# Who makes the low parts of the seven quarter products: three subtractions per unit moved from GpSimd to VectorE

## The reference

```
x = x + 0.5 * (silu(h @ w_gate) * (h @ w_up)) @ w_down      h = rms_norm(x), w_gate and w_up 1024 x 2816
proj = h @ w_in ; x = x + (gate_a * branch_a + gate_b * branch_b) @ w_out
x = x + 0.5 * (silu(h @ w_gate) * (h @ w_up)) @ w_down      second feed-forward block, weights of its own
```

## Time and profile before

| | |
|---|---|
| median of three runs | 2593.43 us (2591.48 to 2594.05) |
| the profiled execution | 2593.64 us, its span 2591.8 us |
| PE busy | 2576.2 us, 99% of the span |
| DVE busy | 1408.8 us, 54% |
| ACT busy | 1147.6 us, 44% |
| POOL busy | 1122.9 us, 43% |

### The profile page before, as it was taken

How to read it: one execution, slowest core, us unless ns; L and a number is a source line. 1 busy time by engine, 2 the same in 40 slices (tenths; PEclk the granted TensorE clock), 3 DMA queues, 4 the chain that set the end, 5 groups by cost and what they waited for, 6 DMA issues and landing times.

```text
span 2591.8 us, 32921 instructions
## 1 busy us (share of the span) xinstructions
PE 2576.2 (99%) x13244; PEld 2165.6 (84%) x13244; DVE 1408.8 (54%) x1949; ACT 1147.6 (44%) x1691; POOL 1122.9 (43%) x458
## 2 busy tenths in 40 slices
PE   9999999999999999999999999999999999999999
PEld 7999887888876788988888988878888778898987
DVE  7777426751345357665187682458423453677630
ACT  5334336743546443334243342467445464433331
POOL 4434544455431334435434345434544314434353
PEclk9999999999999999999999999999999999999999
DMA  5322724323322332322324223343233232324232
GB/s 166 118 78 86 235 88 118 106 96 108 94 72 88 102 114 90 112 84 90 99 90 130 86 82 107 92 125 102 86 110 97 66 103 90 122 65 130 66 102 77
DMA packets 258669, 263.77 MB, mean 102 GB/s; under 512 B 9574, under 2 KB 243174, under 8 KB 258518
## 3 DMA queue, kind: packets, MB, share of 16 engines
q1 hardware_dynamic: 253178, 251.65, 31.3%
q10 hardware_dynamic: 5340, 10.02, 1.2%
HBM read 252.25 MB, written 10.57 MB: 101 GB/s over the span
## 4 chain that ended last, share of the span: by engine, by line
PE 90%; DVE 6%; ACT 2%; DMA 1%; issue 0%; ACTq 0%; SPq 0%; DVEq 0%
PE ps L1671 22%; PE ps L1676 22%; PE ps L1675 22%; PE ps L1779 5%; PE ps L1783 5%; PE ps L1784 5%; PE ps L1951 1%; DVE scan L1474 1%; PE ps L2009 1%; PE ps L2024 1%; PE ps L1969 1%; PE ps L1973 1%; PE ps L1974 1%; DVE scan L1466 1%; DVE scan L1471 1%; ACT i_and_r L854 0%
## 5 line engine op out<-in xcount | busy, mean ns | idle before, releaser
L579 POOL TENSOR_TENSOR wlo<-raw,whi 128x1024 fp32r<-128x1024 f32 x386 | 972.6, 2532 | 1032.6 <-ACT whi L623 1032.6
L1671 PE MATMUL ps<-h_lo,whi 128*128 128x512 f32 x1632 | 639.2, 392 | 3.6 <-DVE y L1406 2.8
L1675 PE MATMUL ps<-h_hi,whi 128*128 128x512 f32 x1632 | 636.5, 390 | 0.0
L1676 PE MATMUL ps<-h_hi,wlo 128*128 128x512 f32 x1632 | 636.4, 390 | 0.0
L623 ACT ACTIVATE whi<-raw 128x1024 fp32r<-128x1024 f32 x386 | 403.7, 1053 | 459.1 <-PE ps L1671 404.6
L1671 PEld LDWEIGHTS ps<-h_lo,whi 128*128 128x128 f32 x1632 | 307.4, 188 | 73.3 <-issue 9.2
L1676 PEld LDWEIGHTS ps<-h_hi,wlo 128*128 128x128 f32 x1632 | 307.1, 188 | 64.6
L1675 PEld LDWEIGHTS ps<-h_hi,whi 128*128 128x128 f32 x1632 | 307.4, 188 | 62.7
L1671 PE MATMUL ps<-act_lo,whi 128*128 128x512 f32 x704 | 274.1, 389 | 0.0
L1675 PE MATMUL ps<-act_hi,whi 128*128 128x512 f32 x704 | 273.9, 389 | 0.0
L1676 PE MATMUL ps<-act_hi,wlo 128*128 128x512 f32 x704 | 273.9, 389 | 0.0
(11 more groups left out here) (232 smaller groups left out, 4396.6 us busy)
## 6 DMA issues: line engine op xcount, KB each, us to landing
raw<-in_w_in SPq DMA_DIRECT2D x124, 512.0 KB
raw<-in_w_up SPq DMA_DIRECT2D x88, 512.0 KB
raw<-in_w_down SPq DMA_DIRECT2D x80, 512.0 KB
w_a<-in_w_gate SPq DMA_DIRECT2D x60, 512.0 KB, 5.0
tmp<-in_w_gate SPq DMA_DIRECT2D x20, 512.0 KB, 7.9
rel_band<-rel_rows ACTq DMA_DIRECT2D x1, 8192.0 KB, 39.5
raw<-in_w_up_b SPq DMA_DIRECT2D x16, 512.0 KB
raw<-in_w_out SPq DMA_DIRECT2D x16, 512.0 KB
```

The costliest lines, as they stand in the source:

```text
L579: nc.gpsimd.tensor_tensor(wlo[:, s, :], src, whi[:, s, :].bitcast(F32), ALU.subtract).then_inc(lo_made, 1)
L1671: ins = pe.matmul(ps[:, b, :], w_hi, x_lo, start=start, stop=False)
L1675: pe.matmul(ps[:, b, :], w_hi, x_hi, start=False, stop=False)
L1676: return pe.matmul(ps[:, b, :], w_lo, x_hi, start=False, stop=stop)
```

## The change

VectorE makes the low parts of all seven operands of a unit's quarter products; POOL makes those of the four up chunks alone. A11's low part comes before that of S2, A12's (with the wait for A12's load ahead of it) before that of S1, and A22's after the sum that waits for P5. The counts follow: `sum_lo` steps by seven a unit (PARTS is 7), all seven products wait for it, `lo_made` steps by four, and SP waits for `sum_lo` alone before it loads the next quarters. ACT's two waits in the last unit are for the same two low parts as before under new counts.

```
 SP      if unit:
-            sp.wait_ge(sum_lo, ((2 * l + f) * UNITS + unit) * 4)
-            sp.wait_ge(lo_made, lows[0] - UPS)
+            sp.wait_ge(sum_lo, ((2 * l + f) * UNITS + unit) * PARTS)
...
-        lows[0] += 3
 POOL    for unit in range(UNITS):
-            base = ring[0]
             plain(UPS)
-            lo(w_a11[:, :])
-            ring[0] = base + RING_A12
-            lo(w_a12)
-            ring[0] = base + RING_A22
-            lo(w_a22[:, :])
+            ring[0] += PARTS
 ACT     if last:
-            act.wait_ge(sum_lo, C.now(sum_lo) + 2)
+            act.wait_ge(sum_lo, C.now(sum_lo) + 4)
...
-            act.wait_ge(sum_lo, C.now(sum_lo) + 4)
+            act.wait_ge(sum_lo, C.now(sum_lo) + 6)
 DVE     (two up tiles scaled, unless last)
+            lo_sum(base + RING_A11, w_a11[:, :])
             lo_sum(base + RING_S2, w_s2[:, :])
         (two more up tiles scaled, unless last)
+            dve.wait_ge(held_loaded[3], C.next(held_loaded[3], 16))
+            lo_sum(base + RING_A12, w_a12)
             lo_sum(base + RING_S1, w_s1[:, :])
-            dve.wait_ge(held_loaded[3], C.next(held_loaded[3], 16))
...
             added(u4, p5, u2).then_inc(bank_read[p5], C.made(bank_read[p5]))
+            lo_sum(base + RING_A22, w_a22[:, :])
             if last:
                 act_low(2, 4)
 PE
-    seventh(chunk(), p1, *of_h(low, left))
-    seventh(sum_chunk(sums + 1), p6, *of_t(T2, 1))
...
+    seventh(sum_chunk(sums + 1), p1, *of_h(low, left))
+    seventh(sum_chunk(sums + 2), p6, *of_t(T2, 1))
...
+    seventh(sum_chunk(sums + 7), p4, *of_t(T4, 4))
```

More of the change, by code:

```diff
@@ L751, in ffn @@
                     C.step(sum_made, 4)
-                    C.step(sum_lo, 4)
+                    C.step(sum_lo, PARTS)
                     sums = C.now(sum_made)
@@ L1123, in down_low @@
             def down_low(l, f, n):
-                first = 4 + UNITS * (UPS + 3)
+                first = 4 + UNITS * UPS
                 block = first + (KD // 2) * len(G22)
@@ L1797, in strassen @@
                 p1, p6, p2, p5, p7, p3, p4 = GATE_BANKS
-                seventh(chunk(), p1, *of_h(low, left))
-                seventh(sum_chunk(sums + 1), p6, *of_t(T2, 1))
[L1800 to L1805, removed]
+                seventh(sum_chunk(sums + 1), p1, *of_h(low, left))
+                seventh(sum_chunk(sums + 2), p6, *of_t(T2, 1))
+                seventh(sum_chunk(sums + 3), p2, *of_h(high, left))
+                seventh(sum_chunk(sums + 4), p5, *of_t(T1, 2))
+                seventh(sum_chunk(sums + 5), p7, *of_t(T3, 3))
+                seventh(sum_chunk(sums + 6), p3, *of_h(high, right))
+                seventh(sum_chunk(sums + 7), p4, *of_t(T4, 4))
+                C.step(sum_lo, PARTS)
             def ffn(ends=False, begins=False):
```

## The result

The changed kernel takes 2596.9 us (median of 20 runs, 2595.47 to 2599.29), the kernel before 2592.95 us (median of 20 runs). The ratio is 1.0018, interval 1.0011 to 1.0025: 0.18% slower, where 0.1% faster was forecast. It is the first rival that happened. Its waits came to 6.4 us in the waits view and cost 7.5 us by the starts of matmuls, where 7.6 had been worked out; the mixing blocks gave 1.9 us back. The profiled execution took 2596.20 us with a span of 2594.4.

A forecast was written before the change was run, and what follows sets the result against it. PE, busy 99%, bounds the kernel. In the first unit 4.5 us of wait and slow clock go and 1.25 us come, all else 0: 2593.64 - 3.2 = 2590.4 us; range 2587.0 to 2599.0 us.

The forecast's parts named there:

- first rival: Last units: POOL breaks into VectorE's run, PE waits 1.9 us four times, 7.6 us, giving 2598.0 us; chance 0.17.
- the one on the last units: Last unit of each block: VectorE's run goes through before POOL's turn, so 0 us for all four.
- The tight place: Down projection's fifth tile: low part ready at 254.10, PE takes it at 254.53, room 0.43 us.
- The rival's price: Fifth tile's low part ready at 256.4 instead of 254.10: PE waits 1.9 us, four times, 7.6 us.
- The first unit: First block's first unit: wait and slow clock of 4.5 us go, 1.25 us come, 3.2 us gained.
- second rival: First unit: the holds on VectorE are not POOL's, so P6 starts 2.9 us later, 2596.5 us; chance 0.08.
- First units of the other blocks, middle units, loads: VectorE's added low parts fit the room there and loads stay ahead of use: 0 us.
- The fourth rival: Slow-clock stretches at 444.80 and in the second layer don't occur, 3.4 us each: 2587.0 or 2583.6 us; chance 0.10.

The follow-up runs named there:

- e3: Changed kernel with POOL held before each block's first down chunk until VectorE has made the low parts of act tiles 2 and 3; 2589.47 us, ratio 0.9988.
- e10: Changed kernel with the four L1077 of act tiles 0 to 3 in one run right behind A22's low part; 2600.36 us, ratio 1.0035.
- e1: Changed kernel with A22's low part back on POOL, A11's and A12's staying on VectorE; 2589.84 us, ratio 0.9989.

## Why the prediction was wrong

**The step that failed** is the one on the last units, in its words "So a run of DVE already under way isn't broken". It was inferred from one instruction (and three like it in the other blocks) and carried over to another run. Seven kernels show it broken there, and e3, where POOL can't ask before the run is over, has no wait there and comes out near the forecast: 2589.5 us measured, 2590.4 forecast for the change. The tight place, the order of events and the point from which it decides (0.43 us) were right in the text, but under the rival, with a chance of 0.17.

The trace of the kernel before had rows that spoke against the step, and they were not weighed. The argument against the rival was that in the first unit POOL had been waiting already when DVE was held. Timelines of VectorE and POOL, kernel before:

```profile
47.69 1.22 DVE L1171 TENSOR_TENSOR w_s<-w_a 128x1024 f32<-128x1024 f32 x1
48.94 3.29 DVE L1174 TENSOR_TENSOR w_s<-w_s,w_a 128x1024 f32<-128x1024 f32 x1
47.99 3.16 POOL L579 TENSOR_TENSOR wlo<-raw,whi 128x1024 fp32r<-128x1024 f32 x1 [8.18 <-ACT whi L623]
...
532.45 0.69 DVE L1084 TENSOR_TENSOR ya_lo<-tmp,ya_hi 128x512 fp32r<-128x512 f32 x1
533.17 2.77 DVE L1481 TENSOR_TENSOR tmp<-y,scan 128x512 f32<-128x512 f32 x1
532.71 2.68 POOL L579 TENSOR_TENSOR wlo<-raw,whi 128x1024 fp32r<-128x1024 f32 x1 [6.62 <-ACT whi L623]
```

At 47.99 POOL came from 8.18 us without work and asked in the middle of L1171, 0.92 us before its end, and the next instruction, L1174, was held. At 532.71 it asked 0.43 us before the end of a L1084, as at 257.27, and the next one was held too, 2.77 us where it takes 0.69. In both, VectorE's next instruction started 0.03 us after the end of the one before. Without such a pause it was the same in the L1191 (four at 0.60 us would take 2.5 us):

```profile
82.98 9.10 DVE L1191 TENSOR_TENSOR act_raw<-act_raw,gates 128x512 f32<-128x512 f32 x4
88.40 2.54 POOL L579 TENSOR_TENSOR wlo<-w_a,whi 128x1024 fp32r<-128x1024 f32 x1 [0.26 <-ACT whi L623]
```

At 88.40 POOL asked 0.3 us before the end of one L1191, after 0.26 us without work, and the next L1191 took 2.88; so it went at the end of all sixteen units that are not a block's last. These rows show the rival's turn outside the last units.

The Trainium skill (page "SBUF — State Buffer", section "Who interferes with whom") has the shared pair as an exclusive lock, held for the whole instruction by whoever issued first (the words on the whole instruction stand there beside VectorE's 2-port modes). Read instruction by instruction, this gave the rival, and the seven traces and the rows above agree with that reading; the rows at 257.27 before and at 255.93 in e10 still do not. A row that disagreed with a rule at one place was no evidence against it at another.

**The rival's price**, 1.9 us a junction, was right. The waits view shows 1.59 of it, as it counts from the modelled end of the matmul before. By starts, the fifth tile's first matmul would have begun at 254.53 - 3.08 = 251.45, began at 253.21, and a few matmuls later PE stood 1.9 us behind. The turns fell as described: L1077 held until 243.1 and 245.9, POOL's third chunk on the last scaling. On the forecast's axis (3.1 us added) the fifth tile was ready at 256.2 where 256.4 was worked out. The clock did not fall at the junctions of the changed kernel. The windows view of the kernel after:

```profile
253.00:256.50 3.50, 3.29 (x14) 2.74 (x15) 3.50 (x7) 3.50 (x7) 0.26 (x1) 1.00 0.45 149
```

**The first unit** was right in each term: the holds were POOL's (second rival out), P1 began 1.19 us later than before (57.97 against 56.78) for 1.25, and there was no slow clock. One reading at the start of the prediction was wrong, without effect: the list of PE's waits has four entries over 1 us and not three. L1832 waits 2.2 us for POOL's `ones_head` in the first microseconds, and does so in the kernel after as well (L1828, 2.2).

**First units of the other blocks, middle units, loads: 0 forecast, 0 measured.** No product waits there in the waits view after. In the middle units VectorE even ends earlier: the sums of the second unit began at 86.60 instead of 92.01. Of these 5.4 us, 3.1 are the first unit's gain, and the rest is that POOL's A11 no longer holds one of the L1191.

**The fourth rival, and the sum.** By the start of the same matmul in both profiled executions, the changed kernel stands at -3.1 us at 247, -1.2 at 260 (first junction), -2.8 at 455, -0.9 at 1195 (second), +1.0 at 1545 (third), -2.1 at 1735, +1.2 at 1820, +0.7 at 2100 and +2.6 at 2580 (fourth). Each junction cost 1.9 us there, 7.5 in all. The steps in between are the mixing blocks: behind the wait on L1890 the slow stretch was half as long at 444 and missing at 1728, 1.6 and 3.1 us gained, as the fourth rival has it. In the first layer the gain stayed (-2.8 from 455 to the second junction). What the rival missed is that it need not be kept: in the second layer it was lost again. Windows of the kernel after; the first row answers to a stretch that had run at 0.51 before, the second to one at 1.00:

```profile
1728.30:1735.20 6.90, 6.73 (x30) 5.20 (x31) 3.70 (x6) 6.75 (x12) 1.04 (x1) 1.00 0.34 102
1812.00:1816.90 4.90, 4.83 (x14) 3.89 (x15) 4.73 (x7) 4.88 (x7) 1.49 (x1) 0.65 0.01 2
```

PE came earlier to the end of the recurrence, waited 2.55 us for it, until 1812.07 (L1402), instead of 1.14, and the clock fell there: 3.0 us were given back (from -1.8 to +1.2). At 2072 another 0.5 us were gained, as a wait of 0.5 us on L2009 did not come. In e1 3.2 us were gained at 440 to 455 and 3.0 given back at 525.

## What to carry to other kernels

Two engines that hold each other up are priced by who stands behind whom, not by how much work they have: a subtraction of 1.2 us cost 1.9 us of PE time at each junction, since it moved two others behind POOL's turn, and one wait for POOL took it all away (e3). Where an edit frees an engine, work out what it starts earlier and which instruction of its neighbour it then meets. If that neighbour has little room (0.43 us here, beside 2.4 us of POOL's instruction), hold the freed engine back or leave the work where it was. Before a row is used for a rule, look through the same trace for rows of the same kind: 47.99, 88.40 and 532.71 were there to be found. A queueing rule read off one row is a rival, not a term of the sum, until another place of the trace shows it.

## What the runs showed of the hardware that I had not expected

Where POOL asks in the middle of a VectorE instruction with two SBUF operands, it had the next turn in seven kernels at this place, in all four blocks (instructions of 0.68 us took 2.9 behind it). In the runs of L1077 from the fifth tile on it waited 0.9 to 1.8 us instead, and why the two differ is not known: the length of the instruction, the moment of the request and the place in the run were each tried. POOL's own instruction lost 0.02 to 0.4 us in the first case. TensorE's clock fell after a wait of 1.5 us in some executions and not in others: at 1728, behind the same wait, it was 0.51 before and 1.00 after, 3 us at one place. Such a gain need not reach the end: the next wait for a slower chain took it back in the changed kernel at 1812 and in e1 at 525, and did not in the changed kernel's first layer.
